# Experts in order of token count on the chip, two token groups instead of three for eleven of them, and second-layer weights as two rows a partition

## The reference

```
logits = h @ w_router + b_router
top_val, top_idx = top_k(logits, 4);  gate = softmax(top_val)
for each expert e, on the tokens xb that chose it:
    hc  = xb @ w1[e] + b1[e]                    # 1024 -> 2048
    glu = min(hc[:, :1024], 7);  lin = clip(hc[:, 1024:], -7, 7)
    act = glu * sigmoid(1.702 * glu) * (lin + 1)
    y   = act @ w2[e] + b2[e]                   # 1024 -> 1024
out[token] += gate * y                          # over its four experts
```

## Time and profile before

| | |
|---|---|
| median of 3 runs | 1911.57 us (1911.1 to 1913.37) |
| profiled execution | 1912.25 us, of it a span of 1910.4 |
| PE matmuls | 1804.0 us, 94% of the span, 16998 instructions |
| PE weight loads | 998.1 us, 52% (beside the matmuls) |
| DVE, ACT, POOL | 448.2, 409.9, 112.1 us |
| DMA | 505.55 MB, mean 265 GB/s over the span |
| mean granted clock of PE | 0.976 |

### The profile page before, as it was taken

How to read it: one execution, slowest core, us unless ns; L and a number is a source line. 1 busy time by engine, 2 the same in 40 slices (tenths; PEclk the granted TensorE clock), 3 DMA queues, 4 the chain that set the end, 5 groups by cost and what they waited for, 6 DMA issues and landing times.

```text
span 1910.4 us, 39074 instructions
## 1 busy us (share of the span) xinstructions
PE 1804.0 (94%) x16998; PEld 998.1 (52%) x16998; DVE 448.2 (23%) x804; ACT 409.9 (21%) x682; POOL 112.1 (6%) x219
## 2 busy tenths in 40 slices
PE   7999999999999995999999999999999999999980
PEld 6767687888788773343443434434344343443430
DVE  4264425425544444310100101000010000100005
ACT  4474232324334323010010100101001010010102
POOL 0021000000000020000000000000000000000005
PEclk9989999999999997999999999999999999999995
DMA  6201221224234235899999999999999999999936
GB/s 229 86 1 56 93 89 59 69 93 152 92 127 159 84 89 192 324 374 402 389 393 402 381 401 385 395 400 381 400 386 391 402 379 400 387 393 401 387 127 237
DMA packets 123467, 505.55 MB, mean 265 GB/s; under 512 B 10528, under 2 KB 22832, under 8 KB 90544
## 3 DMA queue, kind: packets, MB, share of 16 engines
q1 hardware_dynamic: 100288, 461.40, 61.9%
q0 software_dynamic: 8208, 28.62, 4.7%
q10 hardware_dynamic: 14912, 14.69, 2.2%
HBM read 487.89 MB, written 16.78 MB: 264 GB/s over the span
## 4 chain that ended last, share of the span: by engine, by line
PE 90%; DVE 3%; DMA 3%; ACT 2%; POOL 1%; issue 1%; ACTq 0%; SPq 0%; DVEq 0%; POOLq 0%
PE ps L1600 35%; PE ps L1624 17%; PE ps L1336 8%; PE ps L1338 8%; PE ps L1337 8%; PE ps L1413 1%; PE ps L1566 1%; PE ps L1591 1%; PE ps L1576 1%; PE ps L1403 1%; PE ps L1440 1%; PE ps L1459 1%; PE ps L409 1%; DVE work L1318 1%; PE ps L1615 1%; PE ps L421 1%
## 5 line engine op out<-in xcount | busy, mean ns | idle before, releaser
L1600 PE MATMUL ps<-ring,moe 128*32 128x512 f32 x6144 | 667.3, 594 | 0.0
L1600 PEld LDWEIGHTS ps<-ring,moe 128*32 128x32 f32 x6144 | 185.9, 110 | 463.2 <-issue 457.1
L1624 PE MATMUL ps<-ring,moe 128*32 128x256 f32 x6144 | 337.1, 379 | 0.0
L1624 PEld LDWEIGHTS ps<-ring,moe 128*32 128x32 f32 x6144 | 183.9, 110 | 141.3
L1274 DVE TENSOR_SCALAR moe<-ps 128x768 f32<-128x768 f32 x32 | 30.7, 958 | 953.0 <-PE ps L1600 953.0
L928 DVE TENSOR_TENSOR wl<-raw,wh 128x1024 fp32r<-128x1024 f32 x104 | 126.5, 1225 | 297.3 <-ACT wh L627 297.3
L627 ACT ACTIVATE wh<-raw 128x1024 fp32r<-128x1024 f32 x104 | 109.3, 1058 | 284.6 <-PE ps L1338 283.7
L855 ACT ACTIVATE moe<-ps 128x768 f32<-128x768 f32 x32 | 26.0, 811 | 628.5 <-DVE moe L1274 628.5
L1336 PE MATMUL ps<-oph,wh 128*128 128x512 f32 x384 | 150.5, 392 | 1.6 <-DVE work L1060 1.6
L1338 PE MATMUL ps<-oph,wl 128*128 128x512 f32 x384 | 149.5, 389 | 0.0
L1337 PE MATMUL ps<-opl,wh 128*128 128x512 f32 x384 | 149.5, 389 | 0.0
(11 more groups left out here) (246 smaller groups left out, 1403.3 us busy)
## 6 DMA issues: line engine op xcount, KB each, us to landing
ring<-in_w_exp_in SPq DMA_DIRECT2D x256, 1024.0 KB, 5.8
ring<-in_w_exp_out SPq DMA_DIRECT2D x128, 1024.0 KB, 6.7
raw<-in_w_in SPq DMA_DIRECT2D x26, 1024.0 KB, 5.1
y_main<-moe ACTq DMA_DIRECT2D x128, 96.0 KB, 5.4
raw<-in_w_ckv SPq DMA_DIRECT2D x8, 1024.0 KB, 5.1
raw<-in_w_ret_o SPq DMA_DIRECT2D x4, 1024.0 KB, 5.0
raw<-in_w_mix_out SPq DMA_DIRECT2D x4, 1024.0 KB, 5.1
raw<-in_w_cq SPq DMA_DIRECT2D x4, 1024.0 KB, 5.1
```

Of the source, the lines that this page charges most:

```text
L1600: ins = nc.tensor.matmul(ps[32 * s:32 * s + 32, j, :], x_t[:, k, 32 * j:32 * j + 32], w[:, s, :, :], start=False, stop=(k == KT - 1), tile ...
L1624: ins = nc.tensor.matmul(y_bank(s, j), act_t[:, a, j, q, :], w[:, a, s, :], start=False, stop=(q == W2 - 1 and a == 1), tile_position=(0, ...
```

## The change

- **Order.** On the chip DVE ranks the experts by token count, largest first, with expert 0 put at the first place whatever its count (its weights are loaded before the routing is known). It writes the order into `order`, from which SP, POOL and DVE read expert numbers into registers (`expert_at`).
- **Group sizes.** The first 21 places keep three groups (96 tokens), the last 11 get two (64 tokens). They are processed as place 0, place 31, and then ten cycles of two large experts and one small: 3, 3, 2.
- **Loops.** The loops of PE, ACT, DVE, POOL and SP now run over cycles, each with three experts written out. The order on PE within an expert is the old one. SP reads four places at the head of each cycle.
- **Second-layer chunks.** A chunk is 256 consecutive rows, rows 2p and 2p + 1 in partition p, so one piece of 8 KB. To match, the activations are written with even and odd channels apart (strided reads of PSUM in `gate_silu` and `swiglu`).
- **Result rows.** `y_main` is two parts, 96 rows for each large and 64 for each small expert; the row numbers of the final fetch come from the rank's place (two lookups instead of one). An expert with more than its room would go to the overflow branches as before.
- **Small moves.** The bias selector of the second layer is waited for separately; ACT's copy of the third group comes first and only where there is one.

Added lines of the new prologue on DVE and the new loops, cut to the core:

```diff
-CAP = 96
-GR = CAP // 32
+GR = 3
+CAP = 32 * GR
+SMALL = 11
+BIG = NE - SMALL
+CYCLE = (3, 3, 2)
+CYCLES = (NE - 2) // 3
+LOW = 64
...
+def groups(p):
+
+    return (3, 2)[p] if p < 2 else CYCLE[(p - 2) % 3]
+
+
+def sorted_place(m, i):
+
+    return (m * 2 + 1, m * 2 + 2, m + BIG)[i]
...
-    y_main = nc.dram_tensor("y_main", [NE * CAP, D], F32, kind="Internal").ap()
+    y_main = nc.dram_tensor("y_main", [BIG * CAP + SMALL * LOW, D], F32, kind="Internal").ap()
+    y_big, y_small = y_main[0:BIG * CAP, :], y_main[BIG * CAP:BIG * CAP + SMALL * LOW, :]
...
-            w2 = w_exp_out[0, bass.ds(e, 1), :, :].rearrange("o (a p) n -> p (o a) n", p=P)
-            return w2[:, 2 * (c - W1):2 * (c - W1) + 2, :]
-
-        def ring_slot(c):
-            return ring[:, c, :] if c < W1 else ring[:, c, :].rearrange("p (a n) -> p a n", a=2)
+            q = c - W1
+            return w_exp_out[0, bass.ds(e, 1), 2 * P * q:2 * P * q + 2 * P, :].rearrange("o (p a) n -> p (o a n)", a=2)
...
+            def refill(p, now, after=None):
+
+                for c in range(EC):
+                    if c < W1 and after is None:
+                        continue
+                    sp.wait_ge(w_used, p * EC + (DP + c - 3))
+                    load(after if c < W1 else now, c)
+
+            sp.wait_ge(order_ready, 1)
+            second, third = expert_at(NE - 1), expert_at(1)
             for c in range(W1):
                 sp.wait_ge(w_used, DP + c + 1)
-                load(1, c)
-            with sp.Fori(1, NE - 1) as e:
-                for c in range(EC):
-
-                    sp.wait_ge(w_used, e * EC + (DP + c - 3))
-                    load(e + (1 if c < W1 else 0), c)
-            for c in range(W1, EC):
-                sp.wait_ge(w_used, (NE - 1) * EC + (DP + c - 3))
-                load(NE - 1, c)
+                load(second, c)
+            refill(1, second, third)
+            with sp.Fori(0, CYCLES - 1) as m:
+                four = [expert_at(sorted_place(m, i)) for i in range(3)] + [expert_at(sorted_place(m + 1, 0))]
+                for i in range(3):
+                    refill(m * 3 + (2 + i), four[i], four[i + 1])
+            four = [expert_at(sorted_place(CYCLES - 1, i)) for i in range(3)] + [None]
+            for i in range(3):
+                refill(NE - 3 + i, four[i], four[i + 1])
...
+            def step(p, old, e, g):
+
+                pool.wait_ge(xt_made, p + 2)
+                pool.wait_ge(idx_out, p + 3)
+                pool.wait_ge(sel_used, p + 1)
+                pool.sem_inc(bias_turn, 1)
+                bias_on(old, e)
+                gather_rows(g)
...
+            def x_keep(n, g):
                 act.wait_ge(xt_made, n + 1)
-                nc.scalar.activation(x_t.rearrange("p (b k) n -> p b (k n)", b=2), ps[:, 6:8, 0:4 * CAP], ACT.Copy).then_inc(xt_kept, 1)
+                nc.scalar.activation(x_t(g).rearrange("p (b k) n -> p b k n", b=2),
+                                     ps[:, 6:8, 0:4 * CAP].rearrange("p b (k n) -> p b k n", k=4)[:, :, :, 0:32 * g], ACT.Copy).then_inc(xt_kept, 1)
...
-                nc.scalar.activation(glu_s, ps[:, 0:GR, 0:256], ACT.Silu, scale=ALPHA).then_inc(s_ready, 1)
+                nc.scalar.activation(glu_s[:, 0:g], ps[:, 0:g, 0:256].rearrange("p j (n a) -> p j a n", a=2), ACT.Silu,
+                                     scale=ALPHA).then_inc(s_ready, 1)
...
+                if g > 2:
+                    nc.scalar.activation(y_sb[:, 2, :], ps[:, 5, 0:256], ACT.Copy).then_inc(y_third, 1)
...
+            key, base, shift = names["key"], names["base"], names["shift"]
+            chain(nc.vector.scalar_tensor_tensor(key, names["cnt"], float(NE), iota[:, 0:NE], ALU.mult, ALU.subtract))
+            chain.wait()
+            chain(nc.vector.tensor_scalar(key[:, 0:1], key[:, 0:1], float(2 * T * NE), None, ALU.add))
+            chain.wait()
+            chain(nc.vector.tensor_tensor(larger, key.unsqueeze(1).to_broadcast([P, NE, NE]), key.unsqueeze(2).to_broadcast([P, NE, NE]),
+                                          ALU.is_gt))
+            chain.wait()
+            chain(nc.vector.tensor_reduce(place, larger, AX.X, ALU.add))
+            chain.wait()
+            chain(nc.vector.tensor_tensor(holder, iota[0:1, 0:NE].unsqueeze(2).to_broadcast([1, NE, NE]),
+                                          place[0:1, :].unsqueeze(1).to_broadcast([1, NE, NE]), ALU.is_equal))
+            chain.wait()
+            chain(nc.vector.tensor_tensor(holder, holder, iota[0:1, 0:NE].unsqueeze(1).to_broadcast([1, NE, NE]), ALU.mult))
+            chain.wait()
+            chain(nc.vector.tensor_reduce(order_f, holder, AX.X, ALU.add))
+            chain.wait()
+            nc.vector.tensor_copy(order, order_f).then_inc(order_ready, 1)
+            dve.wait_ge(order_ready, 1)
+            choose(expert_at(NE - 1), groups(1))
...
+            chain(nc.vector.tensor_scalar(shift, place, float(BIG), float(CAP - LOW), ALU.is_ge, ALU.mult))
+            chain(nc.vector.tensor_scalar(place_n, place, float(BIG), 0.0, ALU.subtract, ALU.max))
+            chain(nc.vector.tensor_scalar(base, place, float(CAP), None, ALU.mult))
+            chain.wait()
+            chain(nc.vector.scalar_tensor_tensor(base, place_n, float(LOW - CAP), base, ALU.mult, ALU.add))
+            chain(nc.vector.tensor_tensor(slot, slot, shift.unsqueeze(1).to_broadcast([P, TT, NE]), ALU.add))
+            chain.wait()
             for j in range(1, BLK):
-                chain(nc.vector.tensor_scalar(slots[:, :, j * NE:(j + 1) * NE], slot, -1.0 - CAP * j, None, ALU.add))
+                chain(nc.vector.scalar_tensor_tensor(slots[:, :, j * NE:(j + 1) * NE], sel, 4.0 * T, slot, ALU.mult, ALU.add))
...
+            choose(expert_at(1), CYCLE[0])
+
+            def looked_up(dst, table):
+                chain(nc.vector.tensor_tensor(oh2, oh, table.unsqueeze(2).to_broadcast([P, TT, TOPK, NE]), ALU.mult))
+                chain.wait()
+                chain(nc.vector.tensor_reduce(dst.rearrange("p (t k) -> p t k", t=TT), oh2, AX.X, ALU.add))
+                chain.wait()
+
+            rk, rowf = names["rk"], names["rowf"]
+            chain(nc.vector.tensor_tensor(slot, rank, base.unsqueeze(1).to_broadcast([P, TT, NE]), ALU.add))
+            chain(nc.vector.tensor_tensor(rank, rank, shift.unsqueeze(1).to_broadcast([P, TT, NE]), ALU.add))
+            chain.wait()
+            looked_up(rowf, slot)
+            looked_up(rk, rank)
...
+            with dve.Fori(0, CYCLES - 1) as m:
+                for i in range(3):
+                    swiglu(m * 3 + (2 + i), CYCLE[i], m * 3 * EC + ((2 + i) * EC + UPS))
+                    dve.wait_ge(x_in, m * 48 + (16 * i + 64))
+                    index(m * 3 + (4 + i), CYCLE[(i + 2) % 3])
+                    choose(expert_at(sorted_place(m + 1, i)), CYCLE[i])
...
+                xt = x_t(g)
                 for k in range(KT):
                     pe.wait_ge(w_ring[k], n * 16 + 16)
                     w = ring[:, k, :].rearrange("p (g s n) -> p s g n", g=2, s=4)
-                    for j in range(GR):
+                    for j in range(g):
                         for s in range(4):
-                            ins = nc.tensor.matmul(ps[32 * s:32 * s + 32, j, :], x_t[:, k, 32 * j:32 * j + 32], w[:, s, :, :],
+                            ins = nc.tensor.matmul(ps[32 * s:32 * s + 32, j, :], xt[:, k, 32 * j:32 * j + 32], w[:, s, :, :],
                                                    start=False, stop=(k == KT - 1), tile_position=(0, 32 * s), skip_group_check=True)
...
+            def step(p, i, to_turn=True, to_index=True):
+
+                up(p, CYCLE[i], p * 2 + 1)
+                if to_turn:
+                    x_turn(p + 1)
+                if to_index:
+                    index(p + 2, CYCLE[(i + 2) % 3])
+                down(p - 1, CYCLE[i - 1], p * 2)
+                act_turn(p, CYCLE[i], p + (2 if to_turn else 1))
+
+            with pe.Fori(0, CYCLES - 1) as m:
+                for i in range(3):
+                    step(m * 3 + (2 + i), i)
+            step(NE - 3, 0)
+            step(NE - 2, 1, to_index=False)
+            step(NE - 1, 2, to_turn=False, to_index=False)
+            down(NE - 1, CYCLE[2], 2 * NE)
```

More of the change, by code:

```diff
@@ L262, in layer_kernel @@
         table = names["tabi"][0:1, :].bitcast(U32)
+        order = names["ord"][0:1, :].bitcast(U32)
         n_over = names["nov"][0:1, :].bitcast(U32)
+        larger = w_(4096, NE * NE).rearrange("p (e f) -> p e f", e=NE)
+        holder = work[0:1, 5120:5120 + NE * NE].rearrange("p (e f) -> p e f", e=NE)
+        place = w_(6144, NE)
+        place_n = w_(6176, NE)
+        order_f = work[0:1, 6208:6208 + NE]
         OB = (BLK - 1) * NE
@@ L555, in _ @@
             pool.wait_ge(idx_out, 1)
[L556 removed]
+            gather_rows(groups(0))
             pool.wait_ge(xt_made, 1)
             pool.wait_ge(idx_out, 2)
[L559 to L573 removed]
+            gather_rows(groups(1))
```

(47 more changed lines are left out.)

242 lines of the change are left out of this document (119 added, 123 removed).

## The result

The changed kernel takes 1863.74 us (median of 4, 1862.04 to 1865.71), the kernel before beside it 1912.47 (1911.1 to 1913.5): ratio 0.9746, 95% interval 0.9729 to 0.9763. It gains 48.7 us where 84 were forecast, and 1863.7 lies above the range of 1798 to 1856. The direction was right, the size was not.

The account below looks back on a forecast made before the run. PE bounds the old kernel, DMA 3 to 4% behind; DMA then rules at 31.8 us an expert. The last first layer ends 82.6 us earlier, the tail saves 3.9, less 2 for gaps: 84.5 off 1912.25, so 1828 (range 1798 to 1856).

Parts of the forecast that it names:

- the mixed stretch: Second-layer chunks, row gather and y store moving together: 12.1 us an expert with 8 KB runs, 13.8 at 362 GB/s.
- The end that was held unlikely, 1878: Upper end if 8 KB runs gain nothing: 1.7 us an expert, 50 us more, 1878 us.
- The bound after the change: Expert stage: DMA becomes the bound, 95.4 us a cycle against 91.3 of PE; chance 0.64.
- Rival C: PE stalls at the loop's head, 5.4 us plus 1.4 of clock: cycle of 98.1, total 1852 us; chance 0.15.
- 4.1 us of PE's slack: PE's slack in each cycle against the DMA, taken to hide a code-fetch stall of 0 to 5.4 us.
- PE's saving: A small expert saves PE 10.99 us and costs 23.1; a cycle takes 91.3 us against 102.3.
- Where the last expert's first layer ends: End at 1751.7 instead of 1834.3, 82.6 us less; the tail behind it is 3.9 us shorter.
- The sort: DVE's ranking before the first gather: 7.4 us plus a register read, delaying PE by 0 to 1.0, taken as 0.
- The reads of the order in the loops: Register reads on SP, POOL and DVE: cost nothing; with a shallow queue up to 3 us a cycle.
- B: PE stays the bound if queues sustain 440 GB/s or more: 91.3 us a cycle, 1791 us; chance 0.12.
- D: PE's clock falls for good in small experts' first layers: 162 us more, 1990 us; chance 0.03.
- E: A small expert over 64 tokens takes its own pass, at least 34.1 us; chance 0.02.

Follow-up runs that it names:

- the pairs: Changed kernel with sixteen instead of eleven two-group experts, in cycles of 3, 2 instead of 3, 3, 2: 1841.56 us, ratio 0.9635.
- the kernel where PE rules: Changed kernel with three groups for all 32 experts, its order, loops and layout kept: 1968.75 us, ratio 1.0294.
- the pairs with the old layout: The kernel in cycles of 3, 2 with second-layer weights again as two 4 KB runs a partition and unstrided PSUM reads: 1845.84 us, ratio 0.9665.

## Why the prediction was wrong, point by point

**The step that failed is the DMA's cost of the mixed stretch, "I take 12.1, since what arrives is then the row's own shape".** The forecast laid the 362 GB/s of the earlier trace rows to the 4 KB runs of the second layer and the small packets of the y store. The second was a misreading: that window holds no y store. Neither is the cause: the layout is worth under 0.2 us an expert and the packets nothing that can be told. It is for the most part the gather. Scaled from 64 rows to the 85 of a mean expert of the changed kernel, its cost is 1.65 to 1.76 us, where the forecast's bytes gave it half of 0.70 MB / 362, 0.97: 0.7 to 0.8 short, 20 to 24 us over 30 experts (an estimate; its size was measured on the pairs). Code packets add 0.54 MB / 9 = 0.06 MB an expert, 4 us in all by bytes. An expert cost the queues 33.0 us against 31.8, 36 us over 30; the 8 to 12 that are left stay open. The rest of the forecast's sum holds: 792 + 30 x 33.0 + 5.7 = 1787.7, where the last expert's first layer ended at 1788.8. The end that was held unlikely, 1878, was nearer to the truth in its size though not in its reason, which was the length of the runs; the range left it out.

**The bound after the change.** Right: the queues. A pass without stops still takes the queues' time, and waits for chunks come. But they come late and small in the changed kernel, since the stop holds PE back to almost the same pace.

**Rival C and the price of the loop.** Its working (5.4 + 1.4) was near: 4.9 of stop and 2.6 of clock. The rule of the Trainium skill quoted in the forecast ("Runtime: NRT & Kernel Launch", "Instruction fetch mechanics") agreed: 2304 instructions stop, 1584 and 860 don't. It is hidden, as the forecast took it, but not by the "4.1 us of PE's slack": the stop and its clock take 7.5 of PE, and only since the queues are slower than forecast is the slack 99.0 - 91.3 = 7.7. Had the queues kept to 95.4, PE's 98.8 would by these sums have set the pace, as C says. In the kernel where PE rules, the loop's stops account for the 56 us.

**PE's saving.** Right: 91.3 us a pass forecast, 91.5 seen bare in the kernel with half traffic and no loop.

**Where the last expert's first layer ends.** Forecast 1751.7, and behind it a tail 3.9 shorter. Timeline of the changed kernel, answering to the earlier trace rows, and its start of the stage, to the earlier trace rows:

```profile
754.57 0.42 DVE L1269 TENSOR_TENSOR moe<-work 128x256 bf16<-128x256 f32 x1 [1.05 <-issue]
755.04 0.59 PE L1682 MATMUL ps<-moe 128*64 128x1 bf16 x8 [8.47 <-DVE moe L1269]
760.06 1.54 PE L1692 MATMUL ps<-ident,moe 96*128 96x96 f32 x8 [4.43 <-DMA moe<-h_rows,moe]
...
1788.77 0.51 PE L1742 MATMUL ps<-bias_b,sel_c 96*32 96x256 bf16 x12
1803.89 0.40 PE L1742 MATMUL ps<-bias_b,sel_c 96*32 96x256 bf16 x8 [3.22 <-ACT moe L916]
```

The second layer behind it begins at 1788.77, where the kernel before has 1834.34: 45.6 us earlier instead of 82.6. From there to the span's end it is 71.8 us against 76.1, 4.3 shorter: the tail was right.

**The sort.** Right at cost 0. The pick (the second expert's one-hot matrix) at 754.57 stands behind an idle of 1.05 us, which is the read of the order into a register (bounded by 0 and 3.36 in the forecast), and the index matmuls end at 755.6. PE then still waits 4.43 us for the gather; its turn starts at 760.06 (759.30 before). What holds it there is not the sort but the store and the gather behind it: in the kernels with chunks of 8 KB beside the store it lands in about 16.5 us, in the pairs with the old layout in 11.80. The 0.8 itself says little, since the store's start alone scatters from 738.0 to 742.3 over the traces.

**The reads of the order in the loops.** Right at cost 0: the DMA share stays at 1.02 from 1000 to 1300, so the queues did not run empty behind SP's reads.

**Rivals B, D, E.** B needed 440 GB/s; even with a fifth of the gathered rows the queues reach 415 in the mean. D: the clock doesn't fall for good. It is at half behind each stop (0.50 in every microsecond from 1211 to 1217, 0.72 in the next), PE having stood since 1207.45; in the small expert's first layer, 1181 to 1195, it is at 1.00. Where PE starves it can dip for a short while: in the pairs it stands at 0.66 or 0.67 in seven stretches of 5 us between 800 and 1780, one of them, 1165 to 1170, behind a wait of 2.00 us for a chunk, and is back at 1.00 in between. E: no pass of its own for an overflow appears.

## What to carry to other kernels

When two resources lie within a few per cent, the mixed stretch of the one that becomes the bound has to be taken apart before its rate is credited to a size of run: an indirect gather beside a full weight stream may cost twice its bytes (it did here), and the first thing to try is fewer gathered rows, not longer runs. A row of the profile is credited to a kind of transfer only after the queues of its own window have been read; the 362 had no y store in it. Lengthening a loop body on PE past what stays in place costs a stop and a slow start in each pass. The period of two (1584 instructions) has neither; how much of its 22 us over the period of three comes from that is not shown, since it also gathers fewer rows. Where two sums agree with the measured period, remove each in turn and both at once; a trace alone can't choose.

## What the runs showed of the hardware

- A loop body of 2304 instructions on PE fetches 11 code packets a pass and stops PE at its head for 4.5 us in the mean (2.8 with half the weight traffic, 4.4 with a body of 2580), and the clock is at 0.50 for the first 5 us of work behind it, which costs 2.6; bodies of 860 and 1584 fetch nothing.
- A gather of 4 KB rows beside the weight stream costs 1.24 to 1.32 us for 64 rows where its bytes take 0.62, at a DMA share of 1.02 all the while; slices of 7.5 us fall from 421 GB/s to 351 to 366 with 64 or 96 rows, and to 390 to 401 with 16.
- Runs of 8 KB instead of two of 4 KB, beside another queue's store, delay that store from 11.8 to 16.5 us, and speed the stage by less than 0.2 us per 4 MB; stores of 1 KB packets cost no more than those of 2 and 3 KB (1841.6 and 1840.4 us).
- Reading a value from memory into a register on DVE took 1.05 us of idle.
